# 192 unused bytes in front of the experts' tokens in a one-core hybrid transformer layer

## The reference, cut to what matters

```python
def _expert_choice(h, router, w_gate, w_up, w_down):
    ...
    g, idx = lax.top_k(jnp.swapaxes(aff, 1, 2), cap)
    ...
    xin = h[bidx, idx_flat].reshape(B, N_EXPERTS, cap, D)
    a = jnp.einsum('becd,edf->becf', xin, w_gate)
    b = jnp.einsum('becd,edf->becf', xin, w_up)
    y = jnp.einsum('becf,efd->becd', jax.nn.silu(a) * b, w_down)
    y = (y * g[..., None].astype(y.dtype)).reshape(B, N_EXPERTS * cap, D)
    return jnp.zeros_like(h).at[bidx, idx_flat].add(y)
```

## Time and profile before

| what | value |
|---|---|
| median of 3 runs | 2223.07 us |
| the profiled execution's own time | 2225.76 us |
| span of the profiled execution | 2223.6 us |
| mean granted TensorE clock | 0.981 |
| TensorE busy | 2129.8 us, 96% |
| TensorE weight loads | 1709.5 us, 77% |
| VectorE busy | 1668.5 us, 75% |
| ScalarE busy | 1160.0 us, 52% |
| experts' matmuls | 4608 of 512 columns, between 1125 and 2214 us |

### The profile page before, as it was taken

One profiled execution on the slowest core, in us unless ns is written; L12 is line 12 of the kernel. 1 busy time (PEld: TensorE's weight loads), 2 busy tenths in 40 slices (PEclk: granted clock), 3 DMA queues, 4 the chain that ended last, 5 costly groups with the idle time before them and its releaser, 6 DMA issues.

```text
span 2223.6 us, 27445 instructions
## 1 busy us (share of the span) xinstructions
PE 2129.8 (96%) x10117; PEld 1709.5 (77%) x10117; DVE 1668.5 (75%) x1720; ACT 1160.0 (52%) x1229; POOL 198.0 (9%) x69
## 2 busy tenths in 40 slices
PE   7999999989999999999399999999999999999998
PEld 2998888866577776688278888888888888888886
DVE  3667765167553898753788988998989889898986
ACT  3521222156400221321167777777777778777784
POOL 0000000000000000300011101111011111011100
PEclk9999999999999999999699999999999999999999
DMA  8134454030111133643589999999999999999993
GB/s 307 58 97 161 137 194 143 38 129 15 21 75 35 42 114 115 208 174 103 196 305 358 381 398 391 380 379 380 390 397 383 378 378 380 401 390 377 380 381 116
DMA packets 183292, 538.34 MB, mean 242 GB/s; under 512 B 15231, under 2 KB 57355, under 8 KB 182708
## 3 DMA queue, kind: packets, MB, share of 16 engines
q1 hardware_dynamic: 172768, 505.67, 60.8%
q0 software_dynamic: 4752, 16.78, 2.9%
q10 hardware_dynamic: 5700, 14.90, 1.7%
HBM read 501.66 MB, written 35.65 MB: 242 GB/s over the span
## 4 chain that ended last, share of the span: by engine, by line
PE 49%; DVE 2%; DMA 0%; issue 0%; ACT 0%; POOL 0%; POOLq 0%
PE p_y L247 5%; PE p_y L249 5%; PE p_a L247 5%; PE p_a L249 5%; PE p_a L248 5%; PE p_y L248 5%; PE p_b L248 5%; PE p_b L249 5%; PE p_b L247 5%; PE p_t L2462 1%; PE p_t L2453 1%; DVE idx_rows L2417 1%; DVE late L2420 0%; DVE vals L2415 0%; DMA g1row<-xn_dram,idx_e 0%
## 5 line engine op out<-in xcount | busy, mean ns | idle before, releaser
L2358 DVE TENSOR_TENSOR r_lo<-ring,r_hi 128x2048 fp32r<-128x2048 f32 x384 | 865.8, 2287 | 62.9 <-ACT r_hi L2317 56.0
L2317 ACT ACTIVATE r_hi<-ring 128x2048 fp32r<-128x2048 f32 x384 | 731.0, 1915 | 154.6 <-PE p_b L249 75.5
L247 PE MATMUL p_y<-r_hi,a_hi 128*128 128x512 f32 x512 | 205.3, 401 | 0.0
L247 PE MATMUL p_a<-r_hi,x_hi 128*128 128x512 f32 x512 | 202.5, 396 | 1.0 <-DVE x_lo L2369 1.0
L249 PE MATMUL p_y<-r_hi,a_lo 128*128 128x512 f32 x512 | 200.0, 391 | 0.0
L249 PE MATMUL p_a<-r_hi,x_lo 128*128 128x512 f32 x512 | 199.8, 390 | 0.0
L248 PE MATMUL p_a<-r_lo,x_hi 128*128 128x512 f32 x512 | 199.2, 389 | 0.0
L248 PE MATMUL p_y<-r_lo,a_hi 128*128 128x512 f32 x512 | 199.2, 389 | 0.0
L247 PE MATMUL p_b<-r_hi,x_hi 128*128 128x512 f32 x512 | 199.2, 389 | 0.0
L248 PE MATMUL p_b<-r_lo,x_hi 128*128 128x512 f32 x512 | 199.2, 389 | 0.0
L249 PE MATMUL p_b<-r_hi,x_lo 128*128 128x512 f32 x512 | 199.2, 389 | 0.0
(11 more groups left out here) (352 smaller groups left out, 3648.5 us busy)
## 6 DMA issues: line engine op xcount, KB each, us to landing
ring<-in_w_gate SPq DMA_DIRECT2D x128, 1024.0 KB, 8.5
ring<-in_w_up SPq DMA_DIRECT2D x128, 1024.0 KB, 8.2
ring<-in_w_down SPq DMA_DIRECT2D x128, 1024.0 KB, 11.8
w_raw<-in_w_in SPq DMA_DIRECT2D x17, 1024.0 KB, 6.2
ada_rest<-in_ada_w SPq DMA_DIRECT2D x16, 1024.0 KB, 5.3
ada<-in_ada_w SPq DMA_DIRECT2D x8, 1024.0 KB, 15.2
gate_dram<-zs ACTq DMA_DIRECT2D x16, 512.0 KB, 2.6
x_normed<-gate_dram SPq DMA_DIRECT2D x16, 512.0 KB, 4.3
```

The costliest lines, as they stand in the source:

```text
L247: pe.matmul(out, a_hi, b_hi, start=start, stop=False)
L2317: act.activation(r_hi[:, i % PARTS], ring[:, i % RAW], ACT.Copy).then_inc(hi_ready, 1)
L2358: dve.tensor_tensor(r_lo[:, i % PARTS], ring[:, i % RAW], r_hi[:, i % PARTS].bitcast(F32), ALU.subtract).then_inc(lo_ready, 1)
```

## The change

A tile of 48 floats (192 bytes in each partition) that nothing uses is declared in front of x_hi. x_hi, x_lo, au, a_hi, a_lo and the small tiles behind them start 192 bytes later, at remainder 384; r_hi, r_lo and xf keep 192. No instruction is added, removed or moved.

```diff
@@ -2219,6 +2219,7 @@
         sb, ps = g["scope"](s)
         r_hi, r_lo = sb("r_hi", [P, PARTS, 2048], F32R), sb("r_lo", [P, PARTS, 2048], F32R)
         xf = sb("xf", [P, 2, 4, P])
+        sb("to_384_bytes", [P, 48])
         x_hi, x_lo = sb("x_hi", [P, KD, P], F32R), sb("x_lo", [P, KD, P], F32R)
         au = sb("au", [P, 2, 512])
         with ExitStack() as below:
```

## The result

The changed kernel takes 2232.56 us (median of 5 runs, 2230.65 to 2235.39), the kernel before 2223.07 us. The ratio is 1.0038, interval 1.0027 to 1.0049: slower by 9.5 us, where 26 us were forecast. The way was right and the size was not: 2232.56 lies under the likeliest case's own range, 2238 to 2269. It lies inside the range of all cases, 2198 to 2264, only because that range reached down to the faster rival. The interval of the ratio leaves 6 to 11 us for the difference.

A forecast was written before the change was run, and what follows sets the result against it. The experts were taken as bound by TensorE's gapless matmuls: 6.4 ns more on 3456 to 4608 of them, 22.1 to 29.5 us, taken as 26, on 2223.1 gave 2249 us; range of all cases 2198 to 2264.

The forecast's parts named there:

- the likeliest case: Expert matmuls get slower with the unequal operand pair: some 26 us more, 2249 us, own range 2238 to 2269, chance 0.48.
- the faster rival: Expert matmuls get faster, as attention's k_context record suggests: 4 ns on 4608, 18 us gained, 2205 us; chance 0.29.
- What bounds the experts: In the experts TensorE has no gap and loads wait for compute; only the matmuls' distance, 227 ns, can change the time.
- No cost on ScalarE and VectorE: Their passes on the moved tiles lie beside matmuls, VectorE having 104 us of each 1000 free; taken as nothing.
- The pair of operands decides: Moving and next stationary operand, read together by TensorE: equal remainders modulo 512 give 227 ns, the merge's unequal pair 233.5.
- The price of the pair: Each expert matmul pays the merge's excess: 6.0 ns by records, 6.7 by distances, taken as 6.4.
- the restart: Matmuls right behind a round of transposes: ten distances from 1172.79 to 1175.10 us take 231 ns each.
- How many matmuls feel it: Between 3456 expert matmuls, those not behind transposes (22.1 us), and all 4608 (29.5 us); taken as 26 us.
- The argument for the size: 227 ns is near the low end of distances seen (restart 231, merge up to 237), so a new offset more probably loses.
- The rival by multiples of 64: Only the remainder of 64 bytes matters; 192 and 384 are multiples, so record 389 ns, 2223 us; chance of same 0.23.

## Why the prediction was right in its way and wrong in its size

- **What bounds the experts.** Right. TensorE stayed without a gap, and the time came from the distance of matmuls alone.
- **No cost on ScalarE and VectorE.** Right, and shown by the run with everything at 384: tokens, activations and au at the very same place, ratio 1.0003.
- **The pair of operands decides.** Right. Difference 0 at 128, 192 and 384 gives 389 ns each; difference 416 gives the merge's records in the experts too.
- **The price of the pair.** This is the step that failed: "I take 6.4", the merge's value, "the only long run of such products with an unequal pair". The prediction spoke of equal and unequal pairs, as if there were two classes. The merge's pair is at 160 modulo 256 and the change's at 192, and the price is a function of that number: 6.7 ns there, 2.2 ns (228.9 against 226.7) here. The lower end of the case's range failed with it. Its least price, 4.3 ns, is the restart's 231 less 226.7, and nothing tied the restart to the price. The restart was also read from one round: behind all 95 rounds of the kernel before, ten distances take 227.5 or 231.3 ns, 228.9 in the mean.
- **How many matmuls feel it.** The count was of the right size: 4418 distances between matmuls that stand next to each other and aren't right behind transposes have a mean of 229.0 ns, where they had 227.2, so 1.9 ns each, 8.3 us. With 4608 and 2.2 ns the prediction's own upper sum is 10.1 us, with 3456 it is 7.6; the 9.5 us measured lie between. That the matmuls behind transposes feel less was right too: their ten distances went from 228.9 to 229.6 ns. The interval of 6 to 11 us is too wide to choose between the two counts.
- **The argument for the size** was that 227 is at the low end of the distances seen, so that a new offset more probably loses. That holds: none of the differences tried is under 0's, and nine of the eleven in the map lie above 230 in the mean. It gave the direction; it couldn't give 192's value.
- **The faster rival** rested on k_context, whose pair has the change's very difference, with a record of 279 against 283 ns. Its number was the only one in the trace at that difference, and it pointed the wrong way. The reason named against it, runs of four matmuls, fits what the experts show: the first four distances behind transposes are 230.1 ns before and 230.6 after the change, 0.5 ns where the steady price is 2.2. But no run gave k_context another difference, so this isn't shown for its stage. No other row of the trace before had a price for 192.
- **The rival by multiples of 64** is out: 64 and 128 are the dear ones. Its sentence from the Trainium skill (TensorE: Matmul & The Clock Gate, "Step-by-step: what each phase is for") says that loading the next weights takes no bandwidth from the running matmul. Here the loads' addresses alone move the matmuls from 226.7 to 234.3 ns, so the measurement speaks against it for float32r operands at the full clock. At the half clock and for plain fp32 passes (379 ns at 416 and at 256) the trace agrees with it.

## What to carry to other kernels

Where TensorE streams float32r matmuls of 512 columns back to back, each with a weight load beside it, make the stationary operand's start equal to the moving operand's modulo 256 bytes in each partition. It costs fewer than 256 unused bytes and was worth up to 7.6 ns of 234 for each matmul. This was seen with tiles cut in steps of 512 bytes or multiples of 1024, so that one difference holds for all matmuls of a product. Read the distance of starts in long runs, by stage, and compare it with the addresses of that stage: a price read at one difference says only that addresses count, not what another difference costs. A short run of such matmuls (some ten or fewer after other work) shows the start and not the steady state.

## What the runs showed of the hardware that was not expected

- The price of an address difference is not monotone: 226.7 ns at 0, 230.7 at 8, 226.7 or 233 at 16, 233.3 at 32, 234.3 at 96, 228.9 at 192 and 233.3 again at 224.
- It has a period of 256 bytes, though a weight load reads 512 bytes of each partition.
- At difference 16 the same code ran in two steady states, 226.7 and 233 ns, in different stretches of one execution, by what went before them; 240 (226.7 and 228.4) and 448 (228.9 and 233.3) have two as well.
- With one of three loads off, two thirds of the full price was paid, most of it in the matmul after the one that the load stood beside.
- Even at the best difference 13.4 ns of each matmul (226.7 less 512/2.4) aren't columns. No run here got under that with these products, and what would is open. So is what inside the chip makes the price: the runs show which number sets it, not why.
